# Prompt routed straight into tokens, its last addition in column halves, samples routed and normalised during the output projection, one gate row inside the first expert unit

## What is computed

```python
y, new = token_mixing(h, lp, ctx)          # ends with merged @ w_out
x = x + g1 * y
h = rmsnorm(x, lp['norm2_g']) * (1 + sc2) + sh2
x = x + g2 * ec_moe(h, lp['w_router'], lp['w_gate'], lp['w_up'], lp['w_down'])
...
def ec_moe(h, w_router, w_gate, w_up, w_down):
    cap = CAPACITY_FACTOR * n // N_EXPERTS          # 16 for the prompt, 32 for the samples
    aff = jax.nn.softmax(jnp.einsum('bnd,de->ben', h, w_router), axis=1)
    vals, idx = lax.top_k(aff, cap)
    xg = jax.vmap(lambda hb, ib: hb[ib])(h, idx)
    a, u = xg @ w_gate, xg @ w_up                   # per expert, 1024 x 1024
    o = ((silu(a) * u) @ w_down) * vals             # and added back to the tokens chosen
```

## Time and profile before

| | |
|---|---|
| median of 3 runs | 1747.46 us (1747.43 to 1747.52) |
| profiled execution | 1747.9 us, its span 1745.8 us |
| PE busy | 1675.4 us, 96% of the span |
| DVE, ACT, POOL busy | 659.5, 310.9, 118.2 us |
| read from memory | 531.29 MB, 306 GB/s over the span |
| granted clock of PE | 1.00 |

### The profile page before, as it was taken

The page is one execution under the profiler, slowest core; times in us unless marked ns, Lnnn a source line. Parts: engine busy times, 40 slices in busy tenths (PEclk is TensorE's granted clock), DMA queues, the critical chain, the costliest instruction groups (busy, mean ns, idle before and its releaser), DMA issues.

```text
span 1745.8 us, 18825 instructions
## 1 busy us (share of the span) xinstructions
PE 1675.4 (96%) x7072; PEld 783.1 (45%) x7072; DVE 659.5 (38%) x1394; ACT 310.9 (18%) x798; POOL 118.2 (7%) x161
## 2 busy tenths in 40 slices
PE   7999999999999998898999999999999999988989
PEld 3456666554333332242345566665553433323323
DVE  2257666676122120121124566666651111211211
ACT  2234322032101010000022432222130100000100
POOL 0251000000000000000012500000000000000000
PEclk9999999999999999999999999999999999999999
DMA  9531333766999999999994224338669999999997
GB/s 394 191 126 32 138 121 128 291 252 266 383 427 427 430 426 428 430 427 427 426 371 147 104 79 141 114 117 340 256 234 413 427 427 429 429 428 428 429 428 333
DMA packets 51410, 534.33 MB, mean 306 GB/s; under 512 B 6096, under 2 KB 7280, under 8 KB 11408
## 3 DMA queue, kind: packets, MB, share of 16 engines
q1 hardware_dynamic: 47520, 523.27, 73.0%
q0 software_dynamic: 2112, 7.97, 1.3%
q10 hardware_dynamic: 1712, 2.20, 0.4%
HBM read 531.29 MB, written 2.13 MB: 306 GB/s over the span
## 4 chain that ended last, share of the span: by engine, by line
PE 79%; DMA 20%; DVE 0%; issue 0%; ACT 0%; SPq 0%; DVEq 0%; ACTq 0%
PE bank L2186 23%; DMA ring<-in_w_moe 19%; PE bank L1763 14%; PE bank L1782 7%; PE bank L1829 7%; PE bank L2223 5%; PE bank L2017 5%; PE bank L1869 2%; PE bank L1929 2%; PE bank L2084 1%; PE bank L1791 1%; PE bank L1904 1%; PE bank L1806 1%; PE bank L1751 1%; PE bank L1754 1%; PE bank L1715 1%
## 5 line engine op out<-in xcount | busy, mean ns | idle before, releaser
L1763 PE MATMUL bank<-hT,ring 128*128 128x384 f32 x768 | 257.7, 489 | 0.0
L2186 PE MATMUL bank<-M,hT 128*64 128x512 f32 x1024 | 228.0, 595 | 16.2 <-DMA M<-in_w_moe 16.2
L2186 PE MATMUL bank<-ring,hT 128*64 128x512 f32 x976 | 220.1, 594 | 9.9 <-DMA ring<-in_w_moe 9.9
L1763 PEld LDWEIGHTS bank<-hT,ring 128*128 128x128 f32 x768 | 142.9, 190 | 99.8 <-issue 8.1
L2186 PEld LDWEIGHTS bank<-M,hT 128*64 128x64 f32 x1024 | 71.6, 137 | 162.8 <-issue 134.9
L2186 PEld LDWEIGHTS bank<-ring,hT 128*64 128x64 f32 x976 | 70.1, 137 | 146.7 <-issue 130.6
L1782 PE MATMUL bank<-M,ring 128*128 128x384 f32 x384 | 132.1, 487 | 0.0
L2186 PE MATMUL bank<-M 128*64 128x512 f32 x512 | 115.5, 595 | 12.9 <-DMA M<-in_w_moe 12.9
L2186 PE MATMUL bank<-ring,M 128*64 128x512 f32 x512 | 115.3, 596 | 12.6 <-DMA ring<-in_w_moe 11.1
L1063 ACT ACTIVATE M<-bank 128x512 f32<-128x512 f32 x32 | 19.1, 597 | 568.3 <-PE bank L2186 568.3
L1829 PE MATMUL bank<-ring,hT 128*128 128x512 f32 (+1 forms) x288 | 117.3, 567 | 1.1 <-DVE hT L1190 1.1
(11 more groups left out here) (252 smaller groups left out, 1549.5 us busy)
## 6 DMA issues: line engine op xcount, KB each, us to landing
ring<-in_w_moe SPq DMA_DIRECT2D x92, 2048.0 KB, 28.6
M<-in_w_moe SPq DMA_DIRECT2D x88, 2048.0 KB, 29.9
ring<-in_w_mix SPq DMA_DIRECT2D x110, 1024.0 KB, 5.2
M<-in_w_moe SPq DMA_DIRECT2D x16, 1024.0 KB, 12.5
arena<-in_w_moe SPq DMA_DIRECT2D x4, 1024.0 KB, 11.7
ring<-in_w_mix SPq DMA_DIRECT2D x4, 576.0 KB, 5.0
arena<-in_bias_rows POOLq DMA_DIRECT2D x4, 512.0 KB, 5.9
g2slot<-in_bias_rows POOLq DMA_DIRECT2D x4, 512.0 KB, 7.3
```

What stands on the lines that cost most here:

```text
L1763: ins = mm(ps[:, 0:TOK], w[:, q, (j % 4) * P:(j % 4 + 1) * P], hT[:, 4 * h + q, :], start=(h == 0 and q == 0), stop=(h == 1 and q == 3))
L2186: ins = mm(bank[b][64 * e:64 * e + 64, :], lhs(e, 4 * h + q), w, start=(h == 0 and q == 0), stop=(h == 1 and q == 3))
```

## The change

1. The prompt is routed without column groups: `route_prompt` takes `hT` as the stationary operand and 16 columns of `wrA` as the moving one, eight products that leave experts on columns and tokens on partitions. The partial sums, their copy and the fold are gone for tile 0. `wrA` is negated, and the softmax is written with a minimum, so that a subtraction goes; ACT's exponent sums its row on the way.
2. The prompt's second half of the last addition is made in two quarters of 256 columns (`add_half`), turned and copied one by one (`turn_quarter`, `turned_quarter`); its squares are summed in halves.
3. The samples are routed, ranked and turned further ahead among the products of the projection. They are normalised there too, for which `merged` is laid out by tiles, as `xn` lies in the same place.
4. The sample gather is split and put among the steps of the prompt.
5. The prompt's choice is compared straight from PSUM (`chosen_prompt`); POOL clears the rest of that tile of `gsel` beforehand.
6. Two of the four prompt gathers and gate row 11 move behind the first half of the first expert unit (`second_half`). SP loads one of the resident halves ahead of that and one behind it.

```diff
+                sp.wait_ge(rstd_ready, NPOW * (l + 1))
+                load_kept(l, 1)
...
+                    if first and j == ND + 1:
+                        wait_full(sp, l, ("modb", 11, 0))
+                        load_kept(l, 0)
...
+                pool.wait_ge(merged_ready, 24 * (l + 1))
+                nc.gpsimd.memset(gsel[:, 0, :], 0.0).then_inc(gsel_zero, 1)
...
+                def add_half(h):
+
+                    ps = wait_full(dve, l, ("wo", 1, 0))[:, 256 * h:256 * h + 256]
+                    lo, hi = 512 + 256 * h, 768 + 256 * h
+                    step(V.tensor_tensor(ps, ps, g1b[:, 0, lo:hi], ALU.mult))
+                    V.tensor_tensor(x[:, 0, lo:hi], x[:, 0, lo:hi], ps, ALU.add).then_inc(x_mixed if h else x_quarter, 1)
...
+                def chosen_prompt():
+
+                    ps = wait_full(dve, l, ("slt", 1))
+                    dve.wait_ge(gsel_zero, l + 1)
+                    V.tensor_tensor(gsel[:, 0, :].rearrange("p (e s) -> p e s", s=SLOTS)[:, :, 0:CP],
+                                    ps[:, 0:4].unsqueeze(2).to_broadcast([P, 4, CP]),
+                                    slotno[:, 0, 0:CP].unsqueeze(1).to_broadcast([P, 4, CP]),
+                                    ALU.is_equal).then_inc(gsel_ready, 1)
...
-                add_mixed(0, 0)
                 top(0, P, TOK, (0, 1, 2, 3))
                 number(2 * P)
-                add_mixed(1, 0)
+                add_mixed(0, 0)
                 slots(0, 1, T)
                 chosen(0, (1, 2))
+                add_half(0)
+                add_half(1)
+                turned_quarter(1)
                 x_variance(0)
...
+                def route_prompt(n, lo, hi):
+
+                    ps = bank[turn(l, ("route", 0))[0]] if lo else begin(l, ("route", 0))
+                    wait_read(pe, l, ("xt", 0, n))
+                    for kb in range(lo, hi):
+                        ins = mm(ps[:, 0:NE], hT[:, kb, 0:P], wrA[:, 0, kb, 0:NE], start=(kb == 0), stop=(kb == 7))
...
+                first_sample(0, 0)
+                route_prompt(0, 0, 4)
+                turn_quarter(0)
+                first_sample(0, 1)
+                turn_quarter(1)
+                route_prompt(1, 4, 6)
+                route_prompt(2, 6, 8)
                 for k in range(2):
                     gate_row(10, k)
...
+                def second_half():
+
+                    prompt(2)
+                    prompt(3)
+                    for k in range(2):
+                        gate_row(11, k)
...
+                            if first and g == 0 and h:
+                                second_half()
                             project(g, b, h, lambda e, kb: xcur[:, kb, 2 * c + e, :])
```

More of the change, by code:

```diff
@@ L2073, in gate_row, with sample, gather_sample @@
                         done(l, ("modb", i, 0), ins)
-                def gather_sample(gr, bs, first=False):
+                def sample(b, i):
+                    kb = 2 * b + i
+                    v = bank[b][:, i * 256:(i + 1) * 256].rearrange("p (e s) -> p e s", s=SLOTS)
+                    for t in (1, 2):
+                        ins = mm(v[:, :, CP:USED], xn[:, t, kb * P:(kb + 1) * P],
+                                 gsel[:, t, :].rearrange("p (e s) -> p e s", s=SLOTS)[:, :, CP:USED],
+                                 start=(t == 1), stop=(t == 2))
+                    return ins
+                def gather_sample(gr, bs):
                     pe.wait_ge(gsel_ready, 3 * (l * NG + gr) + 2)
@@ L2080, in gather_sample, with first_sample, prompt @@
                         for i in range(2):
-                            kb = 2 * b + i
-                            v = bank[b][:, i * 256:(i + 1) * 256].rearrange("p (e s) -> p e s", s=SLOTS)
-                            for t in (1, 2):
-                                ins = mm(v[:, :, CP:USED], xn[:, t, kb * P:(kb + 1) * P],
-                                         gsel[:, t, :].rearrange("p (e s) -> p e s", s=SLOTS)[:, :, CP:USED],
-                                         start=(t == 1), stop=(t == 2))
-                        if first:
-                            ins.then_inc(bank_full[b], 1)
+                            sample(b, i)
+                def first_sample(b, i):
+                    if i == 0:
+                        pe.wait_ge(bank_read[b], in_pair(l, b, 0, 0, 0))
+                        sample(b, i)
+                    else:
+                        sample(b, i).then_inc(bank_full[b], 1)
+                def prompt(b):
+                    ps = begin(l, ("prompt", b))
+                    for i in range(2):
+                        ins = mm(ps[:, i * 64:(i + 1) * 64].rearrange("p (e s) -> p e s", s=CP), xn[:, 0, (2 * b + i) * P:(2 * b + i + 1) * P],
+                                 gsel[:, 0, :].rearrange("p (e s) -> p e s", s=SLOTS)[:, :, 0:CP], start=True, stop=True)
+                    done(l, ("prompt", b), ins)
                 def gather_prompt(gr):
@@ L2135, in _ @@
+                first_sample(3, 0)
                 turn_slots(1, 0, 1)
[L2136 removed]
                 pe.wait_ge(xn2_ready, 3 * l + 3)
                 pe.wait_ge(gsel_ready, 3 * (l * NG + 1))
[L2139 to L2144 removed]
+                prompt(0)
@@ L2146, in pair_step @@
+                prompt(1)
+                first_sample(3, 1)
+                def second_half():
+                    prompt(2)
+                    prompt(3)
+                    for k in range(2):
+                        gate_row(11, k)
                 def pair_step(gr, c, more, last=False, first=False):
```

150 lines of the change are left out of this document (88 added, 62 removed).

## The result

The changed kernel takes 1750.43 us (median of 18 runs, 1750.02 to 1752.7) against 1747.43 (18 runs, 1746.83 to 1748.21): a ratio of 1.0019, interval 1.0011 to 1.0026. That is 3.0 us slower. The interval lies wholly above 1, so the loss is clear of noise; its size lies just inside the 3.5 us (0.2%) that the prediction counts as no change. The forecast was 1750.6, with 1.55 us lost in each layer.

A forecast was written before the change was run, and what follows sets the result against it. The expert weight stream bounds each layer, which ends a constant time after the first 2 MB issue. First product 1.3 us earlier, first unit 2.7 to 2.9 longer: 1.55 per layer, 3.1 in all, 1750.6 us; range 1746.5 to 1753.0.

The forecast's parts named there:

- The projection ends at 427.9.: Layer 0 output projection on PE: end moves from 427.26 by 0.23 for the ranks' turn and 0.4 of waiting.
- The wait ahead of the ranks' turn: PE, among the projection's products: about 0.4 us of waiting for the samples' ranking on DVE.
- 16 narrow records at 0.113, 1.8 us.: PE, eight products routing the prompt: each 16-column record costs a whole stationary tile's 0.113 us, 1.8 us in all.
- Rival 1: Prompt-routing records on PE cost a whole load record, 0.191 us each: 2.5 us per layer, 1752.5 us; chance 0.20.
- rival 2: Narrow prompt-routing products on PE are nearly free: loss only 1.2 us per layer, 1749.9 us; chance 0.10.
- Gate row 10 at 431.35, the first product at 438.6, the half load at 442.3.: Layer 0 on PE and SP: first expert product 1.3 us earlier than before, half load issued at 442.3 against 443.63.
- 2.7 us more inside the first unit, the 2 MB issue at 448.4 to 448.6.: First expert unit, layer 0: two gathers (0.9) and gate row 11 (1.8) delay the 2 MB weight issue from 447.06.
- 1.55 per layer, with a hole in the stream up to 449 and the full rate from 451.: Expert weight stream: restarts 1.55 us later per layer, 3.1 in all, then runs at 428 GB/s.
- Rival 3: Weight stream restarts with the first half's release: 1.3 us earlier per layer, 1744.9 us; chance 0.10.
- rival 4: The weight stream's start does not matter; what the first unit gives it takes back: 1747.5 us; chance 0.10.
- What was costed at nothing: Samples' normalisations, a bank copy moved to ACT, POOL's memset, reordered resident loads, merges' layout and SP's new wait: no cost.

The follow-up runs named there:

- second_half_ahead: Changed kernel with part 6 undone: the two later prompt gathers and gate row 11 put back ahead of the first expert product; 1749.73 us.
- gate11_twice_inside: Changed kernel with the products of gate row 11 made twice inside the first expert unit, ahead of the first 2 MB issue; 1754.03 us.
- kept_in_stream: Changed kernel with only SP's resident half MB load that waits for gate row 11 issued ahead of the fifth weight-waiting load instead of the second; 1753.96 us.
- gate11_later: Changed kernel with gate row 11 moved from the first expert unit to ahead of the third, and its resident half MB load issued later; 1751.40 us.
- covers_narrow: Changed kernel with part 6 undone and the covers dealt out anew, keeping the narrow-record prompt routing; 1746.11 us, ratio 0.9993 to before.
- prompt_by_rows: Changed kernel with part 1 undone: prompt routed by four column groups, a copy and a fold instead of 16 narrow records; 1752.75 us.
- the last three kernels: Changed kernel with part 6 undone and covers dealt out anew: old routing, the same with one sample product moved, narrow routing; 1746.70, 1746.56, 1746.11 us.

## Why the prediction was right

The value, its sign and its mechanism held. Point by point, on the second profile of the changed kernel; it began the projection 0.58 earlier than the profile of before (380.95, 381.53), which I add to the times below:

- *The projection ends at 427.9.* 427.41 + 0.58 = 427.99. The wait ahead of the ranks' turn, set at 0.4, is 0.31 in the first profile (424.05).
- *16 narrow records at 0.113, 1.8 us.* The first eight start at 427.85 and the turn behind them at 428.66: 0.101 a record, 1.6 in all. It is little below the 0.113 and 0.116 of 64 and 128 columns, so the number of columns hardly counts; that agrees with a price set by the stationary tile, as taken, though no run tests that by itself. Rival 1 (0.191) and rival 2 fall by this row. The Trainium skill's "TensorEngine Tiling (Array Packing)", section "Instruction Overhead", has a matmul with one moving column last as long as one with 60; at 60 cycles of 2.4 GHz that is, by my estimate, 0.025 us. The trace does not agree: it shows four times that.
- *Gate row 10 at 431.35, the first product at 438.6, the half load at 442.3.* 431.41, 438.70 and 442.39.
- *2.7 us more inside the first unit, the 2 MB issue at 448.4 to 448.6.* From the first product to the issue it is 448.20 - 438.12 = 10.08 against 7.12 before: 2.96 more, 0.06 above the upper end of what was allowed for changes of form. The issue is at 448.78.
- *1.55 per layer, with a hole in the stream up to 449 and the full rate from 451.* 1.72 and 1.57; the stream moves 102 GB/s in 447 to 449 and 401 in 451 to 453 of the second profile. Rival 3 (the first half's release restarts the stream) falls by second_half_ahead, rival 4 (the start does not matter) by gate11_twice_inside, which cost 3.6 of 3.6.
- *What was costed at nothing* held as far as it shows: from the start of the projection to its end it is 46.46 us in place of 45.73, 0.73 more against the 0.63 forecast, so the samples' normalisations are hidden; and the resident loads cost nothing, because the stream has a hole there. kept_in_stream shows what it costs when that cover goes, 1.3 to 1.8 per layer. SP's new wait for gate row 11 is over at 444.61, 3.59 ahead of the issue behind it.

That the median meets the forecast to 0.2 us is in part luck: the issue came 0.17 later than forecast in layer 0, and the sum of the issues' delays, 3.29, stands 0.3 above the time's 3.0.

One step was incomplete, without harm to the sum: the "two gathers (0.9) and gate row 11 (1.8), 2.7 us of PE that nothing else covers". On the path as the change lays it, yes. But the row itself covers the copies behind the gathers, 0.75, so it is worth only 0.95 when taken out, which I learned from gate11_later.

Where the 1.72 of layer 0 lies is told by PE's busy time from the first product of the projection to the issue, in the kernel before, in the second profile of the changed one, and in covers_narrow:

```profile
381.53:447.06 65.53, 64.32 (x273) 32.26 (x273) 42.09 (x99) 14.26 (x29) 3.62 (x6) 1.00 0.73 284
380.95:448.20 67.25, 65.57 (x271) 33.25 (x271) 40.70 (x94) 15.30 (x35) 3.94 (x7) 1.00 0.72 281
381.01:446.10 65.09, 64.91 (x271) 33.37 (x271) 40.71 (x94) 15.19 (x35) 3.93 (x7) 1.00 0.74 286
```

PE waits 1.21 us of it before, 1.68 in the changed kernel and 0.18 in covers_narrow. So against before the change loses 1.25 by a busier PE and 0.47 by waiting. Of the 1.25 the narrow records make 0.59, since PE is busy for 64.98 us in the same stretch of prompt_by_rows (layer 1, against 65.57); the rest was not taken apart. The 0.47 is about the wait for the copies ahead of the first product (0.46) that part 6 brings. Against covers_narrow, which has the same 271 records, 1.50 of the 2.16 is waiting: the changed kernel leaves uncovered what gate row 11 and the gathers cover in covers_narrow.

## What to carry to other kernels

Where a stream of loads is the bound, ask of each change when the stream starts for good and which bytes travel before that; work on the engine behind that moment is nearly free (here, 1.8 us a layer), and ahead of it costs its full length where it covers no wait. A filler is worth the waits under it and not its own length: before moving one, list the waits at its old place and at its new one, and the loads that are queued on its end. A step that takes more of an engine can still win when it fills that engine's idle time and takes a link out of a chain.

## What the runs showed of the hardware that was not expected

Three of the profiles (the first of the changed kernel, kept_in_stream and prompt_by_rows) have a stretch of some 3 us at a granted clock of 0.50, each beginning near the start of the first expert product of layer 0, and there the first half takes 5.33 to 5.35 us in place of 3.65. It costs 1.7 us: 68.93 to the issue against 67.25. Ahead of it PE had run narrow products with waits between them. But the 4 us up to the first expert product look the same in the first profile, where the clock fell, and in the second, where it stayed at 1.00 (product at 438.94 and 438.12):

```profile
434.94:438.94 4.00, 2.80 (x24) 2.38 (x22) 2.09 (x8) 1.78 (x6) 0.98 (x2) 1.00 0.98 416
434.12:438.12 4.00, 2.80 (x24) 2.38 (x22) 2.08 (x8) 1.77 (x6) 0.98 (x2) 1.00 0.94 397
```

PE is busy for 2.80 us in both, so its activity there does not tell the two executions apart. A mean clock of 0.999 stands beside one or two runs of each kernel that has gate row 11 behind the first expert product (2 of 18 of the changed kernel, 2 of 11 of gate11_later). None of the 62 runs of before whose clock is listed, and none of the last three kernels, shows it; all of these have gate row 11 ahead of the first product; of the eleven runs of second_half_ahead, which has it there too, one averaged 0.999. What decides it in a single execution stays open.
